# A two-layer decoder trunk on one core: six buffers for loaded weight pieces and four for split ones, with splits asked for three pieces ahead

## What is computed

```python
def hybrid_layer(x, ...):
    h = rms_norm(x, norm_g)
    proj = jnp.einsum('bsd,de->bse', h, w_in)
    (q_lat, kv_lat, z_a, dn_qkv, dn_a, dn_b, z_b, dil_qkv, z_c, gate_logits) = split_last(proj, IN_SPLITS)
    y_a = mla_branch(q_lat, kv_lat, ...)
    y_b = gated_deltanet_branch(dn_qkv, dn_a, dn_b, ...)
    y_c = dilated_branch(dil_qkv, ...)
    ys = jnp.stack([y_a * jax.nn.silu(z_a), y_b * jax.nn.silu(z_b), y_c * jax.nn.silu(z_c)], axis=2)
    branch_out = jnp.einsum('bsnc,ncd->bsnd', ys, w_branch)
    gates = jax.nn.sigmoid(gate_logits.reshape(B, S, N_BRANCHES, D_MODEL))
    mixed = jnp.sum(gates * branch_out, axis=2)
    return x + jnp.einsum('bsd,de->bse', mixed, w_out)
```

## Time and profile before

| | us |
|---|---|
| median of 3 runs | 772.14 |
| lowest, highest | 771.51, 772.38 |
| the profiled execution's own time | 771.47 |
| its span, first to last instruction | 769.7 |
| TensorE matmul busy | 755.1 (98%) |
| TensorE weight load busy | 652.9 |
| VectorE busy | 584.0 |
| ScalarE busy | 475.6 |
| GpSimd busy | 179.1 |
| read from HBM | 122.03 MB, 160 GB/s over the span |

### The profile page before, as it was taken

How to read it: one execution, slowest core, us unless ns; L and a number is a source line. 1 busy time by engine, 2 the same in 40 slices (tenths; PEclk the granted TensorE clock), 3 DMA queues, 4 the chain that set the end, 5 groups by cost and what they waited for, 6 DMA issues and landing times.

```text
span 769.7 us, 11699 instructions
## 1 busy us (share of the span) xinstructions
PE 755.1 (98%) x4270; PEld 652.9 (85%) x4270; DVE 584.0 (76%) x844; ACT 475.6 (62%) x1067; POOL 179.1 (23%) x183
## 2 busy tenths in 40 slices
PE   7999999999999999999999999999999999999998
PEld 6999888788887888888899998878888878888886
DVE  6677868988889776776655797789887987667763
ACT  6869585668595654455457768656777856435441
POOL 1165104304231002411032721313050300035100
PEclk9999999999999999999999999999999999999999
DMA  8657636354545445655565564563356545546651
GB/s 244 230 162 219 191 111 188 100 156 138 158 147 180 139 141 169 182 167 192 134 201 179 162 189 136 150 201 115 111 166 163 165 138 164 164 137 191 192 164 55
DMA packets 73039, 124.90 MB, mean 162 GB/s; under 512 B 9757, under 2 KB 17047, under 8 KB 72983
## 3 DMA queue, kind: packets, MB, share of 16 engines
q1 hardware_dynamic: 72560, 124.10, 52.8%
q10 hardware_dynamic: 423, 0.06, 0.0%
HBM read 122.03 MB, written 1.05 MB: 160 GB/s over the span
## 4 chain that ended last, share of the span: by engine, by line
PE 85%; DVE 9%; ACT 3%; issue 2%; DMA 0%; ACTq 0%; DVEq 0%
PE bank L797 22%; PE bank L799 21%; PE bank L798 21%; PE bank L781 3%; PE bank L780 3%; PE bank L779 3%; DVE w_lo L1446 3%; PE bank L937 1%; PE bank L827 1%; PE bank L884 1%; ACT w_hi L1119 1%; PE bank L914 1%; ACT at L1186 1%; PE bank L905 1%; PE bank L932 1%
## 5 line engine op out<-in xcount | busy, mean ns | idle before, releaser
L1446 DVE TENSOR_TENSOR w_lo<-raw,w_hi 128x1024 fp32r<-128x1024 f32 (+4 forms) x240 | 294.8, 1254 | 100.0 <-ACT w_hi L1119 98.5
L1119 ACT ACTIVATE w_hi<-raw 128x1024 fp32r<-128x1024 f32 (+4 forms) x239 | 237.7, 1018 | 76.0 <-PE bank L799 63.8
L797 PE MATMUL bank<-w_hi,hT 128*128 128x512 f32 (+2 forms) x704 | 277.2, 394 | 1.2 <-DVE hT L1497 0.7
L799 PE MATMUL bank<-w_hi,hT 128*128 128x512 f32 (+2 forms) x704 | 270.9, 385 | 0.0
L798 PE MATMUL bank<-w_lo,hT 128*128 128x512 f32 (+2 forms) x704 | 270.5, 384 | 0.0
L797 PEld LDWEIGHTS bank<-w_hi,hT 128*128 128x128 f32 x704 | 132.9, 189 | 26.7 <-DVE hT L1497 1.8
L799 PEld LDWEIGHTS bank<-w_hi,hT 128*128 128x128 f32 x704 | 132.7, 189 | 25.7
L798 PEld LDWEIGHTS bank<-w_lo,hT 128*128 128x128 f32 x704 | 133.0, 189 | 23.2
L1920 POOL TENSOR_TENSOR sm<-sm,tab 128x8 f32<-128x8 f32 (+3 forms) x46 | 53.1, 1155 | 198.0 <-ACT dn L1326 73.2
L1938 POOL TENSOR_TENSOR mixed<-mixed,gate 128x512 f32<-128x512 f32 x12 | 21.1, 1762 | 175.9 <-DVE gate L1467 175.9
L779 PE MATMUL bank<-hT,w_hi 128*128 128x256 f32 x192 | 54.6, 285 | 0.0
(11 more groups left out here) (235 smaller groups left out, 991.1 us busy)
## 6 DMA issues: line engine op xcount, KB each, us to landing
raw<-in_w_in SPq DMA_DIRECT2D x168, 512.0 KB, 3.8
raw<-in_w_branch SPq DMA_DIRECT2D x24, 512.0 KB, 4.1
raw<-in_w_out SPq DMA_DIRECT2D x16, 512.0 KB, 4.2
raw<-in_w_in SPq DMA_DIRECT2D x8, 384.0 KB, 4.8
raw<-in_w_in SPq DMA_DIRECT2D x8, 320.0 KB, 4.1
raw<-in_mla_w_kv_b SPq DMA_DIRECT2D x8, 256.0 KB, 2.8
raw<-in_mla_w_q_b SPq DMA_DIRECT2D x4, 384.0 KB, 3.4
xs<-in_x SPq DMA_DIRECT2D x2, 512.0 KB, 4.8
```

The costliest lines, as they stand in the source:

```text
L797: mm(o, src[0][:, a, tok], hi[:, k, :], start=starts and p == k == 0, stop=False)
L799: last = mm(o, src[1][:, a, tok], hi[:, k, :], start=False, stop=ends(u, p) and k == k1 - k0 - 1)
L1119: av(view(w_hi, q % SPLIT, k1 - k0, n), view(raw, q % RAW, k1 - k0, n), ACT.Copy).then_inc(hi_done, 1)
L1446: tt(view(w_lo, q % SPLIT, k1 - k0, n), view(raw, q % RAW, k1 - k0, n), view(w_hi, q % SPLIT, k1 - k0, n).bitcast(F32), ALU.subtract).then ...
```

## The change

It sets RAW to 6 and SPLIT to 4, so there are two more buffers for loaded pieces and one fewer for split ones, in the same 14 buffers of 1024 floats (raw counts once, split twice). `ahead` uses SPLIT, so the splits are asked for three pieces ahead rather than four. In the opening of the program one split less is asked for: piece 3 (unit 1, p = 1) now follows unit 0.

```diff
-RAW, SPLIT = 4, 5
+RAW, SPLIT = 6, 4
 ASIDE = 1
...
 def build_order():
 
     steps, middle = step_table(), middle_table()
-    order = [(0, ("prep", 0, 0)), (0, ("xT", 0)), (0, ("prep", 0, 1)), (0, ("xT", 1)), (0, ("prep", 1, 0)), (0, ("prep", 1, 1)),
+    order = [(0, ("prep", 0, 0)), (0, ("xT", 0)), (0, ("prep", 0, 1)), (0, ("xT", 1)), (0, ("prep", 1, 0)),
              (0, ("xT", 2)), (0, ("xT", 3)), (0, ("norm",))]
```

## The result

The changed kernel takes 815.54 us (median, 813.80 to 816.17) against 771.89 us for the kernel before in the same comparison (771.51 to 772.38): 1.0562 times as long, 95% interval 1.0543 to 1.0580. The prediction was 813.5 us in a range from 797 to 824.

A forecast was written before the change was run, and what follows sets the result against it. The prediction took TensorE to bound the kernel: 771.5 us plus 34.2 of waits for splits plus 7.2 for the clock gave 812.9, or 813.5 on the median's scale, range 797 to 824.

The forecast's parts named there:

- What bounds the kernel: TensorE, busy 755.1 us, sets the time; no split was late, and ScalarE waited only 8.4 us for loads.
- The rule that piece q is ready when q + 1 was: Whole kernel: queue places keep their time but serve the piece before; stalls sum to 34.2 us.
- the twelve predicted sizes: Stalls at pieces 3 (1.9), 24/144 (0.6), 49/169 (1.9), 56/176 (0.4, left out), 69/189 (5.4), 73/193 (7.2/6.9), 123 (2.4 us).
- piece 73: Second long chain, layer 0: ready at 241.9, wanted at 234.72, a stall of 7.2 us.
- The two long chains: VectorE's work behind units 32 to 35: stalls add in full, 12.6 us in layer 0, 12.3 in layer 1.
- Piece 127: Layer 1 opening: 1.1 us late by the rule, costed at nothing, as six raw buffers remove a 2.46 us load wait.
- piece 123: Layer 1 opening: ready at 396.6 against 394.16 wanted, a stall of 2.4 us.
- The subtraction beside GpSimd: Piece 49, once a layer: the subtraction keeps 2.06 us, stall 1.9; if VectorE got the port pair first, 1.1.
- The clock: Clock falls behind the four longest stalls and nowhere else, 1.8 us each, 7.2 in all; bounds nothing to 3.6 each.
- Rival A: The same stalls with the clock kept: 806.3 us, chance 0.24.
- Gains: Piece 3 out of the way early could save at most 0.7 us of TensorE's waits for `hT`; none taken.

The follow-up runs named there:

- the mended one: Also "the mended order": the changed kernel with both long VectorE chains moved and the late small places split earlier; 777.89 us, with four raw buffers 777.61 us.
- the run with the filled stalls: The changed kernel with unneeded TensorE matmuls ahead of the waits for pieces 69, 73, 189 and 193; 807.09 us, ratio 1.0467 to the kernel before.

## Why the prediction was right

- **What bounds the kernel.** TensorE had never waited for a split, and loads were hardly waited for. Both were borne out: the raw buffers alone move nothing, with the late order and with the mended one. ScalarE's waits for loads shrank from 8.4 to 0.4 us, as forecast.
- **The rule that piece q is ready when q + 1 was.** It named every place at which TensorE now stalls, and no other one appeared. Eleven of the twelve predicted sizes are within 0.2 us of the measured step, and piece 73 was put 0.3 too high. Piece 73 came 0.3 sooner because the single subtraction now starts 1.19 us behind the start of its rounding (243.29 to 244.48), and before 1.54 us (229.70 to 231.24). By the rule pieces 4, 5, 25 and 57, and 124, 125, 145 and 177 in layer 1, were short as well, by 0.8 us or less. The prediction does not name them, and each stands right behind a stall that covers it. The run with the order alone shows the rule without any change in buffers.
- **The two long chains add up.** Measured 5.44 and 6.93 in both layers. ScalarE's late eviction, 7.15 us, is the link that was read from the earlier trace rows.
- **Piece 127** was costed at nothing and no step appeared there. Both reasons given were wrong. With four raw buffers there is no step either, and with four and the mended order, where piece 123 is in time and covers nothing, there is none again. The load that came late was that of piece 128, and its wait stays with the piece and not with the place: ScalarE waits 2.42 us for it in that run, against 2.46 before, and none for piece 127. So the rule does not hold at a place whose split was waiting for its own load.
- **The subtraction beside GpSimd** kept its 2.06 us, and the steps at pieces 49 and 169 are 1.95 and 1.97. GpSimd's product had started first again (151.39 against 152.30). The 1.1 that the prediction gives by the Trainium skill, SBUF — State Buffer, section "SBUF: two separate sides", for VectorE first did not come up.
- **The clock.** Predicted 7.2 us in four places at 1.8 "and nowhere else"; measured 8.8 in those four (1.6 to 3.0 each) and 1.3 in a fifth, behind piece 49, where a stall of 1.8 us was not thought to be long enough. The fall was right. Its price was taken from one opening, where the profile shows no granted clock below 1.00 and only the pace was slow. That it came within 2.9 us in all is in part luck. Rival A, without the clock, would have been 806.3; the run with the filled stalls gives 807.09, with one slow stretch of 1.5 us left in it.
- **Gains.** None was counted, and the 0.7 us of waits for `hT` stayed. But 1.6 us came back elsewhere, at pieces 78, 170 and 198, where VectorE and ScalarE had been just too late before. The stalls (35.4 against 34.2) and the clock (10.1 against 7.2) were both put too low, and this gain brings the forecast closer than its terms are.

## What to carry to other kernels

In strictly ordered queues the place at which something is asked for can decide, and not the number of buffers behind it, as it did here between four and five split buffers and between four and six raw ones. Too few still cost: with three raw buffers the kernel was 14 us slower. Before the number is changed, take each place in the producer's queue, see which consumer it will serve afterwards, and compare its end with the consumer's need in the trace of before: here this gave a loss of 44 us to within 3. Where the producer was waiting for its own input, as at piece 128, that wait goes with the item and not with the place. A buffer count that also sets how far ahead work is asked for should be split into two numbers. And a stall of the matmul engine can cost more than its length: behind the four long ones the slower clock cost another 1.6 to 3.0 us each.

## What was not expected of the hardware

A stall of 1.8 us was already followed by the lower clock. TensorE's first matmuls of piece 49 in layer 0 after the change, and three stretches around them:

```profile
154.41 0.50 PE L797 MATMUL bank<-w_hi,hT 128*128 128x512 f32 x1 [1.78 <-DVE w_lo L1446]
...
155.30 0.63 PE L797 MATMUL bank<-w_hi,hT 128*128 128x512 f32 x1
```

```profile
152.00:154.40 2.40, 0.63 (x3) 0.19 (x1) 2.40 (x3) 0.43 (x1) 2.40 (x2) 1.00 0.00 0
154.40:156.00 1.60, 1.59 (x5) 1.30 (x6) 1.60 (x1) 0.00 (x0) 0.86 (x1) 0.72 0.33 35
156.00:159.00 3.00, 3.00 (x9) 2.36 (x9) 2.61 (x3) 0.69 (x1) 0.00 (x0) 0.58 0.58 173
```

The clock falls behind the stall, a matmul that took 0.39 takes 0.63, and the step is 1.3 us. The equal stall in layer 1 (1.80 us ahead of piece 169) had no such step, in this kernel or in the two others with the same order; nor had the 2.3 us ahead of piece 123 after the change. In the run with the filled stalls and in the one with both chains moved it was the other way round: the clock stayed at 1.00 behind 1.78 and 1.82 us at piece 49 and fell behind 2.29 us at piece 123. Up to unit 32 these kernels are the same as the changed one, so at piece 49 it is not the kernel that decides. A stall of about 2 us may or may not cost the clock, and what decides was not tried.

The cost behind nearly equal stalls differs as well: 1.62 us at piece 70 and 3.00 at piece 190, behind 5.28 and 5.27 us. The stretches from the end of each long stall to the return of the clock, in the changed kernel:

```profile
233.84:237.02 3.18, 3.18 (x8) 2.50 (x9) 3.01 (x5) 0.16 (x1) 0.00 (x0) 0.50 0.70 188
255.24:260.90 5.66, 5.66 (x13) 4.46 (x14) 3.48 (x5) 0.69 (x1) 0.00 (x0) 0.50 0.76 269
633.62:639.80 6.18, 6.18 (x15) 4.83 (x16) 3.02 (x5) 2.19 (x9) 0.00 (x0) 0.50 0.76 242
656.40:660.30 3.90, 3.90 (x9) 3.16 (x10) 3.47 (x5) 0.69 (x1) 0.00 (x0) 0.50 0.55 195
```

TensorE works through all four at half the clock, and half of each is 1.6, 2.8, 3.1 and 1.9 us, against steps of 1.62, 2.30, 3.00 and 1.84. The step of 2.30 holds a gain of 0.3 that is there without the slow clock too (-0.31 with the filled stalls). So the price of a fall is here about half the time for which the clock stays down once TensorE works again. Why that time differs between 3.2 and 6.2 us stays open.
